# Scatter-adds of one expert unit issued together, with filler rows of their own

## The reference, cut to what matters

```
y = fourier_mixer(x, w_in, w_out)
h = layer_norm(ALPHA * x + y)
scores = sigmoid(h @ w_router)            # top 2 of the 8 experts of the best group
for each expert e and each token t that chose it:
    out[t] += gate[t, e] * ((silu(h[t] @ w_gate[e]) * (h[t] @ w_up[e])) @ w_down[e])
result = layer_norm(ALPHA * h + out)
```

## Time and profile before

| | us |
|---|---|
| median of 3 runs (2435.72 to 2439.93) | 2438.42 |
| the profiled execution | 2431.16 |
| its span in the trace | 2429.4 |
| start of the first unit's products | 860.27 |
| start of the final norm's loads | 2300.7 |

### The profile page before, as it was taken

One profiled execution on the slowest core, in us unless ns is written; L12 is line 12 of the kernel. 1 busy time (PEld: TensorE's weight loads), 2 busy tenths in 40 slices (PEclk: granted clock), 3 DMA queues, 4 the chain that ended last, 5 costly groups with the idle time before them and its releaser, 6 DMA issues.

```text
span 2429.4 us, 37501 instructions
## 1 busy us (share of the span) xinstructions
PE 2152.7 (89%) x12222; PEld 1819.1 (75%) x12223; DVE 1373.7 (57%) x2253; ACT 1000.2 (41%) x1442; POOL 580.5 (24%) x493
## 2 busy tenths in 40 slices
PE   8999899999998289999999999999999999999600
PEld 3443778878886288998898998899989888989600
DVE  3221258888888546555555555555555555555298
ACT  2221133223332255544545555554554554545243
POOL 1000034444444301111111211112111111121166
PEclk9999999999999589999999999999999999999855
DMA  5980243333433357776776867777677676776386
GB/s 218 288 283 0 81 142 128 123 121 130 143 123 139 121 150 225 200 195 182 209 200 170 240 178 187 223 199 194 185 191 227 177 221 184 193 213 177 74 298 239
DMA packets 136067, 435.59 MB, mean 179 GB/s; under 512 B 30912, under 2 KB 35008, under 8 KB 131904
## 3 DMA queue, kind: packets, MB, share of 16 engines
q1 hardware_dynamic: 98592, 307.12, 38.6%
q0 software_dynamic: 37440, 128.01, 21.4%
HBM read 328.01 MB, written 108.10 MB: 180 GB/s over the span
## 4 chain that ended last, share of the span: by engine, by line
PE 67%; DMA 19%; issue 6%; POOL 4%; DVE 2%; POOLq 1%; ACT 0%; SPq 0%; ACTq 0%; DVEq 0%
PE ps L867 19%; PE ps L749 15%; PE ps L891 12%; DMA sums<-yrow_b,ent_now 6%; DMA sums<-yrow_a,ent_now 6%; DMA xrow_b<-h_rows,ent_in 5%; PE ps L686 5%; POOL fin_r L1655 3%; PE ps L855 3%; DMA sums<-yrow_c,ent_now 3%; PE ps L731 2%; PE ps L705 2%; PE ps L783 2%; PE ps L640 1%; PE ps L899 1%
## 5 line engine op out<-in xcount | busy, mean ns | idle before, releaser
L891 PE MATMUL ps<-wd_hi,hidT 128*128 128x512 f32 x1056 | 302.1, 412 | 0.4 <-ACT hidT L1089 0.4
L1349 DVE TENSOR_TENSOR wd_lo<-wraw,wd_hi 128x1024 fp32r<-128x1024 f32 x132 | 161.8, 1226 | 198.9 <-ACT wd_hi L1047 198.6
L891 PEld LDWEIGHTS ps<-wd_hi,hidT 128*128 128x128 f32 x1056 | 196.8, 195 | 38.3 <-ACT hidT L1089 0.8
L1349 DVE TENSOR_TENSOR wg_lo<-wraw,wg_hi 128x1024 fp32r<-128x1024 f32 x132 | 161.5, 1225 | 92.6 <-ACT wg_hi L1047 92.6
L1349 DVE TENSOR_TENSOR wu_lo<-wraw,wu_hi 128x1024 fp32r<-128x1024 f32 x132 | 160.7, 1218 | 52.3 <-ACT wu_hi L1047 52.2
L867 PE MATMUL ps<-mxT_hi,wg_hi 128*128 128x256 f32 (+1 forms) x1056 | 164.2, 298 | 12.7 <-issue 12.7
L1089 ACT CAST hidT<-hid 128x320 fp32r<-128x320 f32 x132 | 60.6, 459 | 257.3 <-DVE hid L1428 257.3
L867 PEld LDWEIGHTS ps<-mxT_hi,wg_hi 128*128 128x128 f32 x1056 | 150.3, 192 | 17.4 <-issue 15.6
L867 PE MATMUL ps<-mxT_lo,wg_hi 128*128 128x256 f32 (+1 forms) x1056 | 163.1, 297 | 0.0
L867 PE MATMUL ps<-mxT_hi,wg_lo 128*128 128x256 f32 (+1 forms) x1056 | 162.5, 296 | 0.0
L867 PE MATMUL ps<-mxT_hi,wu_lo 128*128 128x256 f32 (+1 forms) x1056 | 161.9, 296 | 0.0
(11 more groups left out here) (210 smaller groups left out, 4106.9 us busy)
## 6 DMA issues: line engine op xcount, KB each, us to landing
wraw<-expert_w_gate SPq DMA_DIRECT2D x132, 512.0 KB, 5.3
wraw<-expert_w_up SPq DMA_DIRECT2D x132, 512.0 KB, 5.6
wraw<-expert_w_down SPq DMA_DIRECT2D x132, 512.0 KB, 3.4
xch<-x SPq DMA_DIRECT2D x16, 1024.0 KB, 6.6
first_stage<-ych SPq DMA_DIRECT2D x16, 1024.0 KB, 8.2
yt<-first_stage SPq DMA_DIRECT2D x16, 1024.0 KB, 4.9
fin_r<-sums SPq DMA_DIRECT2D x32, 512.0 KB, 4.1
out<-fin_r SPq DMA_DIRECT2D x32, 512.0 KB, 2.9
```

The costliest lines, as they stand in the source:

```text
L891: mm = nc.tensor.matmul(psY[h], hidT[:, l, c, t * P:(t + 1) * P], wd[r][:, c, cols], start=(i == c == 0), stop=(i == 2 and c == FC - 1))
L1349: nc.vector.tensor_tensor(piece(1, j), wraw[:, j % SLOTS, :], piece(0, j).bitcast(F32), ALU.subtract).then_inc(wlo_ok, 1)
```

## The change

Part a and b of a unit are scattered without a wait for landing between them, and part c without a wait for b. The wait for both halves (`y_out`) stands once, behind part c and before `ent_now` is overwritten. A landing addition reads its row and writes it back, so two scatters in flight must not hit the same row. Real tokens stand once in an expert's list. The fillers did not: with two sets of 64 they repeated in parts a, b and c. Now there are five sets, one for each list row of a unit (320 filler rows in place of 128 in `sums` and `h_rows`), and the filler of list row r is row 4096 + p + 64 (r mod 5). 65 rows of each list are preset in place of 66.

```diff
-USED_ROWS = S // LANES + 2
+USED_ROWS = -(-S // UNIT) * UROWS
...
-    hd = nc.dram_tensor("h_rows", [S + P, D], F32).ap()
+    hd = nc.dram_tensor("h_rows", [S + UNIT, D], F32).ap()
...
-    acc = nc.dram_tensor("sums", [S + P, D], F32).ap()
+    acc = nc.dram_tensor("sums", [S + UNIT, D], F32).ap()
...
-            sp.dma_start(acc[S:S + P, :], x[0:P, :]).then_inc(pad_out, 16)
-            sp.dma_start(hd[S:S + P, :], x[0:P, :]).then_inc(pad_out, 16)
+            sp.dma_start(acc[S:S + UNIT, :], x[0:UNIT, :]).then_inc(pad_out, 16)
+            sp.dma_start(hd[S:S + UNIT, :], x[0:UNIT, :]).then_inc(pad_out, 16)
...
-            nc.gpsimd.iota(padl.rearrange("p (k h w) -> p k h w", h=2, w=2),
-                           [[0, USED_ROWS // 2], [LANES, 2], [0, 2]], base=S,
+            nc.gpsimd.iota(padl.rearrange("p (k h w) -> p k h w", h=UROWS, w=2),
+                           [[0, USED_ROWS // UROWS], [LANES, UROWS], [0, 2]], base=S,
                            channel_multiplier=1).then_inc(pad_made, 1)
...
                     scatter(t, P, y_out)
-                    own_wait(pool, y_out, 32 * u + 16 * t + 16, pool_gate)
                 with pool.If(wide > 0):
                     own_wait(pool, yc_ok, 2 * u + 4, pool_gate)
                     scatter(2, LANES, yc_out)
                     own_wait(pool, yc_out, 16 * wides_to(pool, u), pool_gate)
+                own_wait(pool, y_out, 32 * u + 32, pool_gate)
```

## The result

The changed kernel takes 2364.11 us (median of 4 runs, 2358.81 to 2369.62), the kernel before 2437.07 (4 runs, 2434.33 to 2439.93). The ratio is 0.9701, 95% interval 0.9674 to 0.9727: faster by 73 us. 2364 was forecast.

What follows compares the result with a forecast made beforehand. PE was taken to bound most, with 81.2 us of loop stalls around its waits for gathered rows. Gains of 73.3 us there and 1.5 at the end, 74.8, off 2438.4 gave 2363.6, rounded 2364; 8-in-10 range 2352 to 2400.

Steps and rivals of the forecast that it cites:

- What bounds: PE bounds the most; in the loop it waits 16 times, 56.5 us, for the next unit's gathered rows, none for weights.
- the clock: In the loop, PE's first transposes and down product run slower behind stalls at a lower granted clock: 22.1 us.
- the sum: All PE stalls in the loop: 56.5 of waits, 22.1 of clock and 2.6 us of unlisted wait, together 81.2 us.
- Who is last: Of the 16 stalls, eight come behind narrow units, where b is the last scatter, and eight behind wide ones, where c is.
- Behind wide units: c is issued 6.5 us earlier, so all stalls there vanish; nothing left over, and 0.5 us for a slow one.
- Behind narrow units: b is issued 3.3 us earlier; five of eight stalls vanish, three keep 4.9 us, plus 2 us spread and 0.5 clock.
- the second rival: Gather moved onto weight loads takes 2 to 3 us longer behind narrow units; 22 us left, time 2378, chance 0.17.
- its signs: Signs of the second rival: gathers of 9 us and more, and stalls of 2 to 3 us behind narrow units.
- the last step of the sum: Profiled 2431.16 less 74.8 gives 2356.4; the runs' median is 7.3 higher, so 2438.4 - 74.8 = 2363.6.
- Scatters in flight: Scatters in flight overlap: a and b hardly meet; b delays c by some 1 us at most in wide units.
- The first rival: Scatters are served one by one, so only the handshake between landing and next issue goes; time 2405, chance 0.12.
- The end and the start: Last unit's b goes earlier on the path to the final norm, 1.5 us gained; larger copies at the start cost nothing.

Runs made afterwards that it cites:

- e8: Changed kernel with the gather issued before the wait for the scatters' landings, and entries loaded before the unit's first weight piece; ratio 0.9599 to the kernel before.
- e12: The kernel of e8 run again, beside the changed kernel on the same chip; 2348.03 us, ratio 0.9636 to the kernel before.
- e2: Changed kernel with only the wait for a's landing before b is issued put back; ratio 0.9778 to the kernel before.
- e3: Changed kernel with only the wait for b's landing before c is issued put back; ratio 0.9852 to the kernel before.
- e11: Changed kernel measured again, without a further change, on the same chip as e12; 2367.01 us, ratio 0.9705 to the kernel before.
- e6: Changed kernel with only the first half of each up-weight piece loaded, so its results are wrong and only time counts; ratio 0.9608 to the kernel before.
- e1: Kernel before with only the new fillers and larger copies at the start, every scatter still waiting for the one before; ratio 1.0012 to the kernel before.
- e4: Changed kernel with a held until b is ready, so both are issued 2 us apart; ratio 0.9804 to the kernel before.
- e7: Changed kernel with the gather of the unit after next issued right behind the last scatter's issue, before the landing waits; ratio 0.9632 to the kernel before.

## Why the prediction was right

**What bounds.** That PE's wait for the gathered rows was the whole of what could be had in the loop, and its worth of 81.2 us with the clock in the profiled execution, is shown: the loops of e8 and e12 have no such wait, and ended within 0.5 us of the sum.

**Who is last.** The waits between a and b and between b and c count where b or c is the unit's last scatter: e2 and e3 took them apart. In narrow units b went at S + 2.2 to 2.5 and c at S + 2.4 to 2.6, as worked out from DVE's rows (2.4 and 2.5).

**Behind wide units:** no wait was forecast to be left, and the six narrow ones have no wait after the change (in e11 one of 1.04 us).

**Behind narrow units** the term was too small. Forecast were 4.9 us in three units, 2 us of spread and 0.5 of clock; the trace after has 13.4 us in eight units and 4.0 of clock, and e11 10.6 and 1.0. The step that was mis-sized is the one that took the path from b's issue to the transposes over from before, 20.1 to 20.7 us in the units that were to fit. It became longer. The eight units with a wait now take 22.6 us for it in the mean, and took 20.7 before. From b's issue to the issue of the gather's part b it is 13.2 us in both; all 1.9 us lie behind that, from the gather's issue to the transposes (9.3 in place of 7.4), since the gather now meets SP's up-weight loads, as e6 shows. Unit 11 shows it best. It had no wait before and was in no term of the prediction, and it has the longest now. POOL's and PE's timelines before (S = 1335.77), where the rows came in time:

```profile
1351.83 0.96 POOL L1602 DMA_INDIRECT xrow_b<-h_rows,ent_in  x1 [0.30 <-issue]
```
```profile
1358.80 0.29 PE L855 MATMUL ps<-cst,xrow_a 128*128 128x128 f32 x1
```

and after (S = 1315.73):

```profile
1331.26 0.97 POOL L1602 DMA_INDIRECT xrow_b<-h_rows,ent_in  x1 [0.30 <-issue]
```
```profile
1341.22 0.42 PE L855 MATMUL ps<-cst,xrow_a 128*128 128x128 f32 x1 [2.30 <-DMA xrow_b<-h_rows,ent_in]
```

That is the second rival's mechanism, just under its size of 2 to 3 us a gather, and its signs came in part: rows that take over 9 us in five of the eight units and stalls of 2.2 to 2.3 us in three. PE's waits are 13.4 us in all where under 10 were named as the sign of being right. With 0.16 for each wait, 18.7 us of stalls are left in this trace and 12.9 in e11's; the forecast left 7.9, the rival 22. Two waits, of 2.30 and 2.18 us, also cost 1.7 and 1.5 us of clock, where 0.1 was taken for anything up to 2.4.

**Why the number was met all the same.** By the traces the loop gained 62.8 us (e11: 68.3), and 73.3 were forecast: 5 to 10 us too much. The medians gained 73.0, 74.8 with the end were forecast, and e11's ratio agrees with the first. One reason is in the last step of the sum. It carried the 7.3 us between the profiled execution and the median over to the changed kernel, as if they had nothing to do with the stalls. But e1's trace shows that slower executions with the old waits have more stalls, 97.3 us in one of 2451.3 us, and e8 and e12, which leave none, gained 97 and 91 us in the medians, more than the 82.7 that the prediction called all there was. So the kernel before had more to gain than its trace showed, and this made up for the gathers that were priced too low. How much of the 7.3 us it was is not shown. The mechanism and its parts were right; that the number was met within 1 us is luck.

**Scatters in flight.** The first rival is refuted by e4. The Trainium skill's rule that POOL's transfers share one queue ("DMA: Bandwidth & Descriptors", "SWDGE vs HWDGE vs iDMA"; the prediction names another section of that page for it) fits the 2.7 us that c loses behind two others, but it does not mean that each waits for the whole of the one before: e4's landings follow each other by 2.6 and 1.7 us, not by 8.

**The end and the start.** The last unit, from the chain of waits after:

```profile
2231.14 0.76 DVE yrow_b L1410
...
2232.68 6.18 DMA sums<-yrow_b,ent_now
```

b goes 1.5 us behind the start of DVE's row in place of 3.2, and lands 6.2 us later in place of 6.0: from that row's start to the landing it takes 7.72 us in place of 9.23, so 1.5 us are gained, as forecast. The time from unit 32's start to the end of the span fell by 174.5 - 173.05 = 1.45 us, but it can't serve as proof, since in e11, the same kernel, it is 174.3. At the start SP issues the two larger copies and is idle until 63.51, as in the earlier trace rows:

```profile
31.64 1.25 SPq L501 DMA_DIRECT2D h_rows<-x  x1
63.51 0.33 SPq L488 DMA_DIRECT2D xch<-x  x1
```

The 2.6 us that the loop starts later are not theirs: e1 and e2, with the same copies, start it at 861.95 and 858.89, on both sides of the 860.27 of before. What makes that start move is open.

## What to carry to other kernels

A wait on an engine that never looks busy can set the pace: POOL was busy for 24% of the span, and its queue held up PE through the order in which it issued. To price such a wait, take the time from the last issue to the use of the data, compare it with the time that the busy engine has, and do it apart for each kind of unit. Expect a transfer that is issued earlier to meet other traffic, and allow it a microsecond or two. And when an issue is moved ahead of one wait, look at once for the next input it needs; here the entries, for which e7's gather waited 9 us, held back a third of the further gain until they were moved too (of the 18.8 us that e8's loop is shorter than the changed kernel's, e7 has 12.5).

## What the runs showed that was not expected

- Three scatter-adds in flight, of 128, 128 and 64 rows of 4 KB, add little to each other's landing: 0.5 us for the second (8.9 to 9.4) and 2.7 for the third (6.2 to 8.9).
- A gather of 128 rows lands 2.0 us sooner (7.7 to 5.7 us) when the four weight loads that run with it are half as large.
- A load of 0.5 to 1 KB of entries takes 6.2 to 6.9 us to land in the median after the change, up to 7.9, and took 3.3 to 4.3 before, without a change to the load itself.
- POOL's copy of the entries takes 0.2 us, but up to 1.3 us when it starts while DVE splits weights: it then ends within 0.1 us of that split, in all 17 such cases of the trace before.
- Two stalls of nearly one length cost very different amounts: behind 2.24 us PE lost 0.1 us, behind 2.30 us 1.7, in the same execution. The granted clock (third column from the right) in the 5 us behind each was 1.00 and 0.66. In e3 1.82 us were enough to cost 1.7.

```profile
963.48:968.48 5.00, 5.00 (x28) 4.38 (x29) 2.62 (x4) 3.38 (x6) 0.19 (x1) 1.00 0.06 21
1341.22:1346.22 5.00, 5.00 (x19) 4.36 (x20) 2.72 (x4) 2.42 (x4) 0.19 (x1) 0.66 0.13 46
```
